# Two networks on one core: TensorE waits for turned columns by halves, for the last turned hidden chunk at the last down slab, and takes the second token tile first in the first down slab

## The chip, the cores and the metric

The kernel runs on one NeuronCore of a Trainium2 chip. The metric is the device time of one execution in microseconds (us); less is better. Engines are named as in the profile: PE is TensorE's matmul, PEld its weight load, DVE is VectorE, ACT is ScalarE, POOL is GpSimd, SP is SyncE, which issues most of the DMAs.

## What is computed

Two residual networks, one after the other, over 256 tokens of width 1024, all in float32. The first has two layers: layer 0 mixes with differential attention and a Fourier branch over latent and context tokens, layer 1 with a gated depthwise convolution. Each is followed by a gated feed-forward network, and shifts, scales and gates come from a condition vector (`ada_w`). The second network has two layers of feed-forward, mixer (short convolution, gated linear recurrence, forgetting attention), feed-forward. What matters here are the six feed-forward networks (width 2816) and the way from each residual sum to the next product:

```python
x = x + gate * swiglu(modulate(rmsnorm(x, g), shift, scale), w1, w3, w2)   # first network, x2
x = x + 0.5 * swiglu_2(rms_norm(x, g), w_in, w_out)                        # second network, x4
def swiglu(h, w1, w3, w2):
    return (jax.nn.silu(h @ w1) * (h @ w3)) @ w2
```

## The kernel before, in words

**Slabs and threes.** All dense weights pass through SBUF as 258 slabs of 128x2048 numbers, in one fixed order. SP loads slab g into one of 5 `raw` buffers as soon as that buffer's last slab has been used up. ACT rounds it to the short format fp32r (`hi`, line 1285), DVE takes the rest (`lo` = raw - hi, line 1803), both into a ring of 4. The split of slab d waits for the semaphore `used` of slab d-4. A product is three matmuls of 512 columns (lines 459 to 461, or 790, 791 and 793 in the down products): hi weights by hi rows, lo by hi, hi by lo. So the rows that are multiplied must be split too: into XTh and XTl (normed input, turned, so that channels lie on the partitions) or HTh and HTl (turned hidden).

**Places.** p = 0 to 9 numbers the residual sums. `down(p)` makes the sums of place p, and the up products of place p read their normed result. There are 256 tokens in two tiles, t = 0 and 1, of 128. An up slab has half of the 1024 input channels for 512 output columns, so a chunk c of 256 hidden columns (gate and up side by side) takes two slabs, 24 matmuls each: 4 blocks of channels, 2 tiles, 3 matmuls. A feed-forward has 11 chunks (NC = 11), 22 up slabs and 11 down slabs; a down slab also has 24 matmuls.

**The up stage** (`ffn`, from line 879). PE multiplies chunk c into banks 0 and 1 or 2 and 3, and between its two slabs turns chunk c-1's hidden rows into bank 4 (`turn_chunk`, line 888, four transposes). ACT makes silu of the gate (line 1566), DVE the hidden product (lines 2238, 2240). From the turned bank ACT makes HTh (line 1546) and DVE HTl (line 1890); the semaphores are `ht_hi` and `ht_lo`. In `down` the sums lie in banks 4 and 5 for tile 0 and in banks 6 and 7 for tile 1 (`acc`), so bank 4, the turning bank, must be free: before the down stage PE waits for `ht_lo` of chunk 9. In down slab 0 it multiplies tile 0 and then tile 1; then `late` turns chunk 10 into bank 2 and waits for its `ht_lo`, although chunk 10 is read only by down slab 10. ACT and DVE have their part of `late` ahead of the split of down slab 4.

**The end of a down stage** (line 804 on). The last three slabs are multiplied for tile 0 first, so DVE can add tile 0's residual while PE does tile 1 of them. DVE and ACT norm the rows, PE turns them (`turn`, line 773), DVE scales them into FULL in two halves of 4 channel blocks (line 2167 or 2170), and ACT and DVE split each half into XTh (line 1301) and XTl (line 1890), with the semaphores `xt_hi` and `xt_lo` for place, tile and half. Then the next up stage begins: in `first_chunks` (places 0 to 3) with two chunks for tile 0, `turn(p, 1)` among them, then both for tile 1; in `first_chunk` (places 4 to 8) with one chunk. Both wait for both halves of a tile's columns before the first product of it, though half 0 of a chunk's slabs reads only half 0 of the columns.

**Other work in the first feed-forward.** In places 0 and 2 the ada weights for later shifts and gates are also loaded through `raw`, quarter by quarter, and DVE sums them over channels into ROW (lines 1837 and 1840, four instructions a quarter). Two quarters later PE turns a half of such a row (`half_turn`, line 518) and DVE stores it (lines 1852 to 1857). In the down stage of the first feed-forward this goes on in `ada_in_down`, after each slab.

Of the kernel before, what the change touches and what calls it, by code (L numbers as in the profile page):

```python
# [27 lines left out]
NC = KF // 2  # L28
# [56 lines left out]
class Counts:  # L85
# [12 lines left out]
    def up(self, name, key=0, step=1):  # L98
        assert (name, key) not in self.table, (name, key)
        shared = SEMAPHORE.get(name, name)  # L100
        self.n[shared] = self.n.get(shared, 0) + step
        self.table[name, key] = self.n[shared]
        return self.sem(name), step
# [182 lines left out]
def program(nc, A, out, known):  # L286

    ctx = ExitStack()
    with ctx:
        counts = Counts(nc, ctx, known)  # L290
        up, at = counts.up, counts.at
# [160 lines left out]
        def tensor_engine(pe):  # L452
# [150 lines left out]
            d = first["w_in"]  # L603
# [170 lines left out]
                                            IDENT[:, :])  # L774
                    last.then_inc(*up("turned", (p, t, h)))

            def down(p, xh, xl, late, order=None, before=None, after=None):
                nslab, d = DOWNS[p][0], first[f"down{p}"]
                order = order or range(nslab)

                def products(s, t):
                    r = (d + s) % RING
                    for n in range(2):
                        kk = 2 * order[s] + n
                        sh, sl = xh[:, kk, tok[t]], xl[:, kk, tok[t]]
                        w = [(hi[r][:, n * D + m * 512:n * D + m * 512 + 512], lo[r][:, n * D + m * 512:n * D + m * 512 + 512])
                             for m in range(2)]
                        begin, end = s == 0 and n == 0, s == nslab - 1 and n == 1
                        for m in range(2):
                            pe.matmul(acc[t][m][:, :], sh, w[m][0], start=begin, stop=False)  # L790
                            pe.matmul(acc[t][m][:, :], sh, w[m][1], start=False, stop=False)  # L791
                        for m in range(2):
                            last = pe.matmul(acc[t][m][:, :], sl, w[m][0], start=False, stop=end)  # L793
                    return last

                for s in range(1 if p == 0 else 0, nslab - 3):
                    ready(d + s)
                    if before:
                        before(s)
                    products(s, 0)  # L800
                    products(s, 1).then_inc(*up("used", d + s))
                    if late is not None and s == 0:
                        late()
                    if after:
                        after(s)
                for s in range(nslab - 3, nslab):
                    ready(d + s)
                    if before:
                        before(s)
                    last = products(s, 0)  # L810
                    if p == 0 and s == 1:
                        late()
                last.then_inc(*up("summed", p))
                products(nslab - 3, 1).then_inc(*up("used", d + nslab - 3))
                if p < 9 and not normed_first(p):
                    turn(p, 0)
                products(nslab - 2, 1).then_inc(*up("used", d + nslab - 2))
                if normed_first(p):
                    turn(p, 0)
                products(nslab - 1, 1).then_inc(*up("used", d + nslab - 1))  # L820

            def first_chunk(p):

                d = first[f"up{p}"]

                def products(half, t):
                    r = (d + half) % RING
                    for k in range(4):
                        kk = 4 * half + k
                        last = three(bank[t][:, :], XTh[:, kk, tok[t]], XTl[:, kk, tok[t]],  # L830
                                     hi[r][:, k * CH:(k + 1) * CH], lo[r][:, k * CH:(k + 1) * CH], kk == 0, kk == KD - 1)
                    return last

                ready(d)
                pe.wait_ge(*at("xt_hi", (p, 0, 1)))
                pe.wait_ge(*at("xt_lo", (p, 0, 1)))
                products(0, 0)
                turn(p, 1)
                ready(d + 1)
                products(1, 0)  # L840
                pe.wait_ge(*at("xt_hi", (p, 1, 1)))
                pe.wait_ge(*at("xt_lo", (p, 1, 1)))
                products(0, 1).then_inc(*up("used", d))
                products(1, 1).then_inc(*up("used", d + 1))

            def first_chunks(p, between, after):


                d = first[f"up{p}"]

                def products(c, half, t):
                    r = (d + 2 * c + half) % RING
                    for k in range(4):
                        kk = 4 * half + k
                        last = three(bank[2 * c + t][:, :], XTh[:, kk, tok[t]], XTl[:, kk, tok[t]],
                                     hi[r][:, k * CH:(k + 1) * CH], lo[r][:, k * CH:(k + 1) * CH], kk == 0, kk == KD - 1)
                    return last

                pe.wait_ge(*at("xt_hi", (p, 0, 1)))
                pe.wait_ge(*at("xt_lo", (p, 0, 1)))  # L860
                for c in range(2):
                    for half in range(2):
                        ready(d + 2 * c + half)
                        products(c, half, 0)
                        if (c, half) == (1, 0):
                            turn(p, 1)
                            after()
                pe.wait_ge(*at("xt_hi", (p, 1, 1)))
                pe.wait_ge(*at("xt_lo", (p, 1, 1)))
                for c in range(2):  # L870
                    products(c, 0, 1).then_inc(*up("used", d + 2 * c))
                    if c:
                        between()
                    products(c, 1, 1).then_inc(*up("used", d + 2 * c + 1))

            def x_groups(c):
# [2 lines left out]
            def ffn(p):  # L879
                f, d = FFNS[p], first[f"up{p}"]  # L880

                def turn_chunk(c, b):
                    pe.wait_ge(*at("hidden", (f, c, 1)))
                    if c:
                        pe.wait_ge(*at("ht_lo", (f, c - 1)))
                    for k in range(2):
                        for t in range(T):
                            last = pe.transpose(b[:, k * S + t * P:k * S + (t + 1) * P], HID[:, t, k * P:(k + 1) * P],  # L888
                                                IDENT[:, :])
                    last.then_inc(*up("hid_turned", (f, c)))  # L890

                def ada_sums(c):

                    gates, shifts = halves_of(FFN_ADA[p][c - 2])
                    for l, mod, h in gates:
                        pe.wait_ge(*(at("added", (p, 1)) if h else at("xt_lo", (p, 1, 1))))
                        half_gate(l, mod, h, bank[5 + h])
                    for l, mod, h in shifts:
                        pe.wait_ge(*at("added", (p, 1)))
                        half_turn(l, mod, h, bank[7])  # L900

                if normed_first(p):
                    first_chunks(p, lambda: turn_chunk(0, bank[4]), lambda: None)
                else:
                    first_chunk(p)
                for c in range(2 if normed_first(p) else 1, NC):
                    if c >= 2:
                        pe.wait_ge(*at("hidden", (f, c - 2, 1)))
                    half_chunk(d + 2 * c, 0, x_groups(c))
                    turn_chunk(c - 1, bank[4])  # L910
                    if p in SHIFTED:
                        ada_sums(c)
                    half_chunk(d + 2 * c + 1, 1, x_groups(c))
                pe.wait_ge(*at("ht_lo", (f, NC - 2)))

                def late():
                    turn_chunk(NC - 1, bank[2])
                    pe.wait_ge(*at("ht_lo", (f, NC - 1)))

                def ada_in_down(s):  # L920

                    for l, mod, h in halves_of(FFN_ADA[0][NC - 2 + s] if s < 2 else DOWN_ADA[s - 2])[1]:
                        half_turn(l, mod, h, bank[1])

                if p in SHIFTED:
                    pe.wait_ge(*at("gate_full", (*FFN_GATE[p], 1)))
                if p == 0:
                    pe.wait_ge(*at("mods", (1, 1, 0, "full")))
                down(p + 1, HTh, HTl, late, after=ada_in_down if p == 0 else None)

            def before_w_out(s):

# [1908 lines left out]
```

## Time and profile before

| | before |
|---|---|
| median of 3 runs | 1772.92 us (1772.43 to 1774.08) |
| profiled execution, span from first to last instruction | 1771.1 us |
| PE busy | 1696.4 us, 96% |
| PEld, DVE, ACT, POOL busy | 1370.1, 1104.2, 807.9, 48.2 us |
| instructions | 20813 |
| DMA | 332.29 MB, mean 188 GB/s |

The time of the profiled execution is given by its span; the median of the runs is 1.8 us above that. Busy time is the sum of the stretches in which an engine ran an instruction; the idle time before an instruction is put down to what released it. Matmuls overlap in the profile (one lasts 0.39 us, but starts come 0.23 us apart), so starts are compared below, not ends.

### The profile page before, as it was taken

How to read it: one execution, taken by the hardware profiler on the slowest of the kernel's cores; microseconds unless marked ns; L12 is line 12 of the kernel's file. 1: busy time of each engine (PE TensorE's matmuls, PEld its weight loads, DVE VectorE, ACT ScalarE, POOL GpSimd, SP SyncE). 2: the span in 40 equal slices, each digit the busy share in tenths (PEclk: the TensorE clock that was granted, in tenths of full speed). 3: DMA queues.
4: the chain of work that ended last, by engine and by line, in shares of the span. 5: the costliest groups of instructions: out<-in, count | busy, mean ns of one | idle time of the engine just before them, and what ended most of it. 6: DMA issues, size and time to landing. Idle time of an engine off the chain costs nothing.

```text
span 1771.1 us, 20813 instructions
## 1 busy us (share of the span) xinstructions
PE 1696.4 (96%) x8168; PEld 1370.1 (77%) x8168; DVE 1104.2 (62%) x1284; ACT 807.9 (46%) x970; POOL 48.2 (3%) x60
## 2 busy tenths in 40 slices
PE   6999899998988999999999999999999999999999
PEld 3775678787656887788787888887888778888877
DVE  3876788877767664655547856554655458755542
ACT  3425544423445443454436555443444346664441
POOL 0001000000000000000001200000000003000000
PEclk9999999999989999999999999999999999999999
DMA  9683288887434765565555427655565454336550
GB/s 354 223 290 113 89 286 281 307 290 257 159 102 152 240 238 179 166 197 184 185 166 167 152 67 212 190 190 177 180 190 190 168 168 164 119 108 210 185 187 25
DMA packets 239985, 332.29 MB, mean 188 GB/s; under 512 B 11024, under 2 KB 191988, under 8 KB 239888
## 3 DMA queue, kind: packets, MB, share of 16 engines
q1 hardware_dynamic: 235872, 321.95, 55.0%
q10 hardware_dynamic: 2704, 5.82, 0.9%
q0 software_dynamic: 1312, 3.19, 0.7%
q8 instruction: 66, 1.08, 0.3%
q14 instruction: 31, 0.25, 0.0%
HBM read 329.87 MB, written 1.05 MB: 187 GB/s over the span
## 4 chain that ended last, share of the span: by engine, by line
PE 84%; DVE 9%; ACT 3%; issue 2%; DMA 1%; SPq 0%; DVEq 0%; ACTq 0%
PE bank L459 17%; PE bank L461 17%; PE bank L460 17%; PE bank L790 7%; PE bank L793 7%; PE bank L791 7%; DVE lo L1803 3%; PE bank L888 2%; DMA raw<-in_ada_w 1%; ACT hi L1285 1%; PE bank L773 1%; PE bank L1229 1%; PE bank L1230 1%; PE bank L1232 1%; PE bank L950 1%
## 5 line engine op out<-in xcount | busy, mean ns | idle before, releaser
L1803 DVE TENSOR_TENSOR lo<-raw,hi 128x2048 fp32r<-128x2048 f32 x258 | 591.2, 2295 | 382.1 <-ACT hi L1285 381.8
L1285 ACT ACTIVATE hi<-raw 128x2048 fp32r<-128x2048 f32 x258 | 491.6, 1911 | 335.5 <-PE bank L461 174.9
L459 PE MATMUL bank<-hi,XTh 128*128 128x512 f32 (+1 forms) x1424 | 564.7, 397 | 9.5 <-ACT XTh L1301 3.0
L461 PE MATMUL bank<-hi,XTl 128*128 128x512 f32 (+1 forms) x1424 | 553.3, 389 | 0.0
L460 PE MATMUL bank<-lo,XTh 128*128 128x512 f32 (+1 forms) x1424 | 552.9, 388 | 0.0
L459 PEld LDWEIGHTS bank<-hi,XTh 128*128 128x128 f32 x1424 | 268.8, 189 | 70.8 <-issue 6.2
L461 PEld LDWEIGHTS bank<-hi,XTl 128*128 128x128 f32 x1424 | 268.3, 188 | 56.0
L460 PEld LDWEIGHTS bank<-lo,XTh 128*128 128x128 f32 x1424 | 268.8, 189 | 52.7 <-issue 1.0
L790 PE MATMUL bank<-hi,HTh 128*128 128x512 f32 x528 | 208.5, 395 | 9.3 <-DVE HTl L1890 9.3
L791 PE MATMUL bank<-lo,HTh 128*128 128x512 f32 x528 | 206.6, 391 | 0.0
L793 PE MATMUL bank<-hi,HTl 128*128 128x512 f32 x528 | 164.0, 392 | 0.0
L790 PEld LDWEIGHTS bank<-hi,HTh 128*128 128x128 f32 x528 | 100.0, 189 | 31.5 <-DVE HTl L1890 11.0
L793 PEld LDWEIGHTS bank<-hi,HTl 128*128 128x128 f32 x528 | 99.7, 189 | 21.0
L791 PEld LDWEIGHTS bank<-lo,HTh 128*128 128x128 f32 x528 | 100.0, 189 | 20.4
L1566 ACT ACTIVATE SG<-bank,ST 128x256 f32<-128x256 f32 x88 | 36.9, 470 | 136.5 <-PE bank L461 136.5
L1840 DVE SCALAR_TENSOR_TENSOR ROW<-raw,CS,ROW 128x512 f32<-128x512 f32 x126 | 94.6, 751 | 4.2
L1301 ACT ACTIVATE XTh<-FULL 128x512 fp32r<-128x512 f32 x44 | 27.4, 632 | 103.2 <-DVE FULL L2170 67.2
L2240 DVE SCALAR_TENSOR_TENSOR HID<-bank,ST,SG 128x256 f32<-128x256 f32 x88 | 38.5, 478 | 55.6 <-ACT SG L1566 55.6
L1890 DVE TENSOR_TENSOR HTl<-bank,HTh 128x512 fp32r<-128x512 f32 x66 | 45.1, 684 | 9.1 <-ACT HTh L1546 9.1
L1566 ACT ACTIVATE SG<-bank 128x256 f32<-128x256 f32 x44 | 14.5, 382 | 71.2 <-PE bank L461 71.2
L1546 ACT ACTIVATE HTh<-bank 128x512 fp32r<-128x512 f32 x66 | 38.5, 583 | 16.3 <-PE bank L888 16.3
L2683 POOL TENSOR_TENSOR hg_e<-hg_BC 128x256 f32<-128x256 f32 x12 | 23.3, 1942 | 635.7 <-DVE hg_BC L2533 615.4
(363 smaller groups left out, 1412.0 us busy)
## 6 DMA issues: line engine op xcount, KB each, us to landing
raw<-in_ffn_w_in SPq DMA_DIRECT2D x176, 512.0 KB, 4.9
raw<-in_ffn_w SPq DMA_DIRECT2D x132, 512.0 KB, 4.9
raw<-in_ada_w SPq DMA_DIRECT2D x96, 512.0 KB, 5.0
raw<-in_ffn_w_out SPq DMA_DIRECT2D x88, 512.0 KB, 4.0
raw<-in_w_mix_in SPq DMA_DIRECT2D x52, 512.0 KB, 4.7
raw<-in_od_pw_w SPq DMA_DIRECT2D x24, 512.0 KB, 5.3
raw<-in_ev_w_in SPq DMA_DIRECT2D x20, 512.0 KB, 9.4
raw<-in_w_mix_out SPq DMA_DIRECT2D x16, 512.0 KB, 3.8
```

Source lines behind the costliest of these rows:

```text
L459: pe.matmul(dst, xh, wh, start=start, stop=False)
L460: pe.matmul(dst, xh, wl, start=False, stop=False)
L461: return pe.matmul(dst, xl, wh, start=False, stop=stop)
L790: pe.matmul(acc[t][m][:, :], sh, w[m][0], start=begin, stop=False)
L791: pe.matmul(acc[t][m][:, :], sh, w[m][1], start=False, stop=False)
L793: last = pe.matmul(acc[t][m][:, :], sl, w[m][0], start=False, stop=end)
L1285: act.activation(hi[r][:, :], raw[g % RAW][:, :], ACT.Copy).then_inc(*up("hi", d))
L1546: act.activation(HTh[:, 2 * c:2 * c + 2, :], b[:, :].rearrange("p (k s) -> p k s", k=2), ACT.Copy).then_inc(*up("ht_hi", (f, c)))
L1566: act.activation(SG[:, t, :], bank[2 * (c % 2) + t][:, 0:HALF], ACT.Silu, scale=1.0 if p in SHIFTED else ST[:, t:t + 1]).then_inc(*up("gat ...
L1803: dve.tensor_tensor(lo[r][:, :], raw[g % RAW][:, :], hi[r][:, :].bitcast(F32), ALU.subtract).then_inc(*up("lo", d))
L1840: m = dve.scalar_tensor_tensor(out=part, in0=w[:, k, :], scalar=CS[:, kk, 0:1], in1=part, op0=ALU.mult, op1=ALU.add)
L1890: dve.tensor_tensor(dst, src, h.bitcast(F32), ALU.subtract).then_inc(*up(name, i))
```

## The change

`down` gets a hook `head`: with it, slab 0 multiplies tile 1, calls the hook, then multiplies tile 0. The feed-forwards give it the wait for chunk 9's `ht_lo`, which stood before `down`. The wait for chunk 10's `ht_lo` leaves `late` and stands before down slab 10. `columns_ready` waits for one half of one tile's columns, and `first_chunk` and `first_chunks` call it before the first product that reads the half. Only PE's program changes.

```diff
-            def down(p, xh, xl, late, order=None, before=None, after=None):
+            def down(p, xh, xl, late, order=None, before=None, after=None, head=None):
...
-                    products(s, 0)
-                    products(s, 1).then_inc(*up("used", d + s))
+                    if head is not None and s == 0:
+                        products(s, 1)
+                        head()
+                        products(s, 0).then_inc(*up("used", d + s))
+                    else:
+                        products(s, 0)
+                        products(s, 1).then_inc(*up("used", d + s))
...
+            def columns_ready(p, t, half):
+
+                pe.wait_ge(*at("xt_hi", (p, t, half)))
+                pe.wait_ge(*at("xt_lo", (p, t, half)))
+
             def first_chunk(p):
...
                 ready(d)
-                pe.wait_ge(*at("xt_hi", (p, 0, 1)))
-                pe.wait_ge(*at("xt_lo", (p, 0, 1)))
+                columns_ready(p, 0, 0)
                 products(0, 0)
                 turn(p, 1)
                 ready(d + 1)
+                columns_ready(p, 0, 1)
                 products(1, 0)
-                pe.wait_ge(*at("xt_hi", (p, 1, 1)))
-                pe.wait_ge(*at("xt_lo", (p, 1, 1)))
+                columns_ready(p, 1, 0)
                 products(0, 1).then_inc(*up("used", d))
+                columns_ready(p, 1, 1)
                 products(1, 1).then_inc(*up("used", d + 1))
...
-                pe.wait_ge(*at("xt_hi", (p, 0, 1)))
-                pe.wait_ge(*at("xt_lo", (p, 0, 1)))
                 for c in range(2):
                     for half in range(2):
                         ready(d + 2 * c + half)
+                        if c == 0:
+                            columns_ready(p, 0, half)
                         products(c, half, 0)
...
-                pe.wait_ge(*at("xt_hi", (p, 1, 1)))
-                pe.wait_ge(*at("xt_lo", (p, 1, 1)))
                 for c in range(2):
+                    if c == 0:
+                        columns_ready(p, 1, 0)
                     products(c, 0, 1).then_inc(*up("used", d + 2 * c))
                     if c:
                         between()
+                    else:
+                        columns_ready(p, 1, 1)
                     products(c, 1, 1).then_inc(*up("used", d + 2 * c + 1))
...
-                pe.wait_ge(*at("ht_lo", (f, NC - 2)))
+
+                def turn_bank_free():
+                    pe.wait_ge(*at("ht_lo", (f, NC - 2)))
 
                 def late():
                     turn_chunk(NC - 1, bank[2])
-                    pe.wait_ge(*at("ht_lo", (f, NC - 1)))
+
+                def last_hidden(s):
+                    if s == NC - 1:
+                        pe.wait_ge(*at("ht_lo", (f, NC - 1)))
...
-                down(p + 1, HTh, HTl, late, after=ada_in_down if p == 0 else None)
+                down(p + 1, HTh, HTl, late, before=last_hidden, after=ada_in_down if p == 0 else None,
+                     head=turn_bank_free)
```

## Rows read from the trace of the kernel before

**Rows 1.** The page's first part: busy time and share of each engine.
```profile
PE 1696.4 (96%) x8168; PEld 1370.1 (77%) x8168; DVE 1104.2 (62%) x1284; ACT 807.9 (46%) x970; POOL 48.2 (3%) x60
```
**Rows 2.** Waits of PE, all of the run: who for whom, us, times, longest.
```profile
PE bank L790 <- DVE HTl L1890: 9.3, 6, 2.2
...
PE bank L459 <- ACT XTh L1301: 3.0, 3, 1.0
...
PE bank L459 <- DVE XTl L1890: 2.6, 2, 1.5
```
**Rows 3.** Timeline of PE, third feed-forward: start us, us, what, [idle before <-releaser].
```profile
868.02 0.39 PE L790 MATMUL bank<-hi,HTh 128*128 128x512 f32 x1
...
873.47 0.60 PE L888 MATMUL bank<-IDENT,HID 128*128 128x128 f32 x4
875.48 0.50 PE L790 MATMUL bank<-hi,HTh 128*128 128x512 f32 x1 [1.41 <-DVE HTl L1890]
```
**Rows 4.** Timeline of PE, chunks turned without a wait after them.
```profile
330.44 0.60 PE L888 MATMUL bank<-IDENT,HID 128*128 128x128 f32 x4
330.87 0.95 PE L518 MATMUL bank<-ONES,ROW 128*128 128x2 f32 x8
...
1083.59 0.60 PE L888 MATMUL bank<-IDENT,HID 128*128 128x128 f32 x4
1083.94 0.48 PE L459 MATMUL bank<-hi,XTh 128*128 128x512 f32 x1
```
**Rows 5.** Timeline of PE, second feed-forward, around `late`.
```profile
680.48 0.50 PE L790 MATMUL bank<-hi,HTh 128*128 128x512 f32 x1 [1.48 <-DVE HTl L1890]
```
**Rows 6.** Timeline of PE, first feed-forward, from the last up product to down slab 2.
```profile
348.36 0.39 PE L461 MATMUL bank<-hi,XTl 128*128 128x512 f32 x1
350.95 0.50 PE L790 MATMUL bank<-hi,HTh 128*128 128x512 f32 x1 [2.21 <-DVE HTl L1890]
...
358.15 0.60 PE L888 MATMUL bank<-IDENT,HID 128*128 128x128 f32 x4
360.17 1.05 PE L518 MATMUL bank<-ONES,ROW 128*128 128x2 f32 x8 [1.41 <-DVE HTl L1890]
361.08 0.48 PE L790 MATMUL bank<-hi,HTh 128*128 128x512 f32 x1
...
368.24 0.95 PE L518 MATMUL bank<-ONES,ROW 128*128 128x2 f32 x8
```
**Rows 7.** Timeline of DVE, the same stretch.
```profile
350.22 0.68 DVE L1890 TENSOR_TENSOR HTl<-bank,HTh 128x512 fp32r<-128x512 f32 x1
...
351.48 2.28 DVE L1803 TENSOR_TENSOR lo<-raw,hi 128x2048 fp32r<-128x2048 f32 x1
353.68 3.10 DVE L1840 SCALAR_TENSOR_TENSOR ROW<-raw,CS,ROW 128x512 f32<-128x512 f32 x4
```
**Rows 8.** Stretches: us, PE, PEld, DVE, ACT, POOL busy, PEclk, DMA share, GB/s.
```profile
352.10:355.50 3.40, 3.40 (x10) 2.62 (x9) 3.33 (x4) 0.65 (x2) 0.00 (x0) 0.50 1.07 382
...
362.40:365.80 3.40, 3.40 (x10) 2.66 (x9) 3.29 (x6) 0.00 (x0) 0.00 (x0) 0.50 0.30 48
...
499.00:512.50 13.50, 8.49 (x24) 5.15 (x23) 7.30 (x13) 9.39 (x21) 0.00 (x0) 0.50 0.29 91
550.10:556.90 6.80, 5.48 (x17) 4.72 (x18) 5.16 (x13) 2.26 (x3) 0.00 (x0) 0.50 0.49 157
748.10:751.50 3.40, 3.40 (x13) 3.01 (x13) 2.85 (x15) 0.80 (x2) 0.00 (x0) 0.50 0.95 290
```
**Rows 9.** Timeline of PE, start of the up products of place 1.
```profile
426.61 0.47 PE L459 MATMUL bank<-hi,XTh 128*128 128x512 f32 x1 [0.54 <-DVE lo L1803]
...
434.24 1.09 PE L773 MATMUL bank<-IDENT,XN 128*128 128x128 f32 x8 [1.90 <-DVE XN L2156]
...
439.12 0.47 PE L459 MATMUL bank<-hi,XTh 128*128 128x512 f32 x1 [1.04 <-DVE XTl L1890]
```
**Rows 10.** Timeline of DVE, place 1: the two halves of tile 1's XTl.
```profile
437.50 1.48 DVE L1890 TENSOR_TENSOR XTl<-FULL,XTh 128x512 fp32r<-128x512 f32 x2
```

## The prediction

> **What bounds the kernel now.** I read the busy shares first: PE 96%, DVE 62% [rows 1]. So time comes off only where PE stands still or runs at its lower clock. The list of PE's waits comes next. HTl, which the first two edits concern, costs 9.3 us in six waits of a down product [rows 2], and 1.4 us in one of line 518 [rows 6]; XTh and XTl, the third edit's, cost 3.0 and 2.6 us [rows 2]. That makes at most 10.7 + 5.6 us of idle time. Third come the timelines at these places, which show what is late next, and last the stretches with the granted clock, which is half (1.2 GHz for 2.4) in some of them [rows 8].
>
> **Edit 1: chunk 10's wait moves from `late` to down slab 10.** In the third feed-forward line 888 starts at 873.47 and the next product at 875.48, 2.01 us; where nothing is waited for it is 0.35 us [rows 3, 4]. The wait costs 1.66 us. The six waits of 9.3 us [rows 2] are this one four times (third to sixth feed-forward, 1.41 each), 1.48 in the second [rows 5] and 2.21 of edit 2: so 4 x 1.66 = 6.64, and 1.73 in the second. In the first, 358.15 to 360.17 is 2.02, less 0.43, the distance of such a pair in its up stage: 1.59 [rows 4, 6].
> What is late next? Down slabs 1 to 3 were split before or during slab 0, and slab 4 is needed three slabs later (5.45 us each, 868.02 to 873.47 [rows 3]). DVE and ACT keep their order, HTl comes first, and it is ready some 40 us before slab 10. Nothing is queued behind the moved wait that needs it earlier.
>
> **Edit 2: tile 1 first, the bank's wait behind it.** It matters only where chunk 9's HTl is late: in the first feed-forward, where the quarters of ada keep DVE busy. There 348.36 to 350.95 is 2.59 us between starts for 0.23 of a steady stream: 2.36 us lost [rows 6]. Now tile 1's 12 matmuls start at about 348.6 and last 2.7, to 351.3, and HTl is finished at 350.90 [rows 7]: all 2.36 us are covered, with 0.4 to spare. In the other five HTl was there already: nothing.
> What the first feed-forward then meets: the turn of chunk 10 comes at about 354.0, and chunk 10's HID is made right behind HTl, before 351.48 [rows 7]. Line 518 follows at 354.5; its row was summed in the up stage. The next line 518, after slab 1, comes at 354.04 + 0.43 + 0.91 + 5.45 = 360.8. It needs the quarter that ends at 356.78 [rows 7], and that DVE has stored the half before: HTl (0.7) from 356.8, `lo` of slab 4 (2.3), two small ones to about 360.1. Only 0.7 us to spare, but enough. From there each DVE step hangs on PE's `used` or on a quarter as before, only earlier.
>
> **Term 3: the clock behind these two stalls.** In the first feed-forward the granted clock is 0.50 from 352.1 to 355.5 and from 362.4 to 365.8 [rows 8]. Slab 0 takes 350.95 to 358.15 = 7.20 us and slab 1 361.08 to 368.24 = 7.16 us [rows 6], against 5.45 at the full clock [rows 3]: 1.75 + 1.71 = 3.46 us. Each fall follows a stall that the edits remove: 2.2 us of idle time, then 1.4 us with the eight tiny matmuls of line 518. Bounds: 0 (both stay or fall elsewhere) and 3.46. I take 3.46, since in the up stage the same pair of lines 888 and 518 without a stall [rows 4] brings no fall.
>
> **Edit 3: columns by halves.** Tile 0 waits at places 0, 1 and 2, three times 1.0 us [rows 2]. With half 0 alone PE starts 0.8 us sooner, but the second slab's products still wait for `lo` (426.61 at place 1), and the turn of tile 1 for XN, with 1.90 us idle [rows 9]. Both are made by DVE, which nothing there makes faster. So this is nothing, at places 0 and 2 too. Places 3 to 8 begin without a stall: nothing. What is left is tile 1 of place 1: PE stands 1.04 us before 439.12 [rows 9], the two halves of XTl take 1.48 from 437.50 [rows 10], the first of them 0.68; it is ready at 438.18, plus the 0.14 that also lies between 438.98 and 439.12: start at 438.32, 0.80 us sooner. What follows (`used`, the split, the biased rows, the gated rows that PE waits for) starts from PE's own signals and comes as much sooner. Bounds: 0 and 1.04; I take 0.80. The extra waits, four in each of nine places, are already satisfied or are those above. Streams that cross slabs, with two to four waits in them, still show 0.23 us between starts, so I count them at nothing; at a guessed upper bound of 0.05 each, 1.8 us.
>
> **The sum.** 6.64 + 1.73 + 1.59 + 2.36 + 3.46 + 0.80 = 16.6 us. The profiled execution's span of 1771.1 becomes 1754.5; the median lies 1.8 above the span, so **1756.3**.
>
> **Rival 1: the clock's low stretches move instead of going.** For it: the falls don't follow stalls in a fixed way. 1.4 us of idle time brings one at 362.4, and the same 1.4 us in the third to sixth feed-forward brings none; others last 3.4 us at 748, 6.8 at 550 and 13.5 at 499, the convolution's end [rows 8]. All that comes after the first feed-forward now comes some 7 us sooner, so the remaining stalls can meet other luck. Against it: at both places the stall itself is gone. It takes 3.46 back: **1759.8**. The Trainium skill (TensorE: Matmul & The Clock Gate, "What's actually happening") says that the monitor behind the clock runs freely and isn't reset when a kernel starts; by that rule falls are drawn anew in each execution, also those at 550 and 748, either way. The trace agrees as far as one trace can: equal stalls, unequal falls.
>
> **Rival 2: the first feed-forward's down stage becomes DVE's or the DMA's.** DMA share is 1.07 at 382 GB/s in 352.1 to 355.5 [rows 8], and a slab with its quarter costs DVE 2.3 + 3.1 of 5.9 us. If PE's lead of 7.4 us (2.36 + 1.59 + 3.46) is taken back there, the time is 1772.9 - 9.2 = **1763.7**. Against it: in 362.4 to 365.8 the DMA share is only 0.30, because SP waited for buffers that DVE freed late; that slack moves the loads forward too.
>
> **Rival 3: the edits do less than they say**, for instance because `late`'s wait is replaced at once by one for slab 1's `lo`, or tile 1 first must wait for banks 6 and 7. Then edit 1's 10.0 us stay: 1772.9 - 6.6 = **1766.3**. Against it: PE waits nowhere for a down slab's `lo` except at places' starts.
>
> **Rival 4, slower: the clock gives out at the starts of places 0 to 3 and in the convolution's end.** Edit 3 gathers idle time: at place 1, 0.99 + 0.54 us become one short stall and one of 1.3 us between small groups of matmuls. If that lets the clock fall there, a low stretch of 3.4 us costs about 1.7 (term 3's 1.75 and 1.71). With those of the first feed-forward kept, 13.1 us of gain are left, so eight more turn the sign, and eleven, 18.7 us, give 1772.9 - 13.1 + 18.7 = **1778.5**. The low stretches listed [rows 8] last 30.5 us, nine such, and PE's idle places at the four starts and in the convolution don't offer room for eleven more.
>
> **How the numbers follow.** Forecast with all terms 0.60, within 1.7 us of 1756.3, a low stretch more or less; rival 1 0.24; rival 2 0.06; rival 3 0.03; rival 4 0.02. The rest, 0.05, is that low stretches at 550 and 748 vanish as well: 1756.3 - 3.4 = 1752.9. The range from 1752.6 to 1761.5 holds the forecast, the last case and rival 1 with a stretch more (1759.8 + 1.7); rivals 2 to 4 stay out. About 0.2%, or 3.5 us, can be told from no change here. All cases but rival 4 are faster by more than that; small mishaps together get 0.02 for no difference.
>
> **What would show it.** In the profile after: no wait of lines 790 and 518 for HTl; starts of line 888 and the next product 0.35 apart in all down stages; slab 0 of the first feed-forward straight after the last up product, and 24 matmuls in 5.45 us there; PEclk 1.00 there; XTl's wait at place 1 down to about 0.2 us; XN's wait at places 0, 1 and 2 at the same end, with longer idle time before `lo`. I am wrong if a new wait of PE over 1 us stands between down slabs, if the first feed-forward's down stage is no 7 us shorter, or if the low stretches add up to as much as before.

## The result, and the profile after

The changed kernel takes 1756.74 us (median of 4 runs, 1754.35 to 1758.85), the one before 1773.50 (4 runs, 1772.43 to 1774.78). The ratio is 0.9906, with a 95% interval of 0.9895 to 0.9918. The forecast was 1756.3. The profiled execution is the slowest of the four: 1758.85 us, with a span of 1757.5.

The page's first part after the change answers to [rows 1]:

```profile
PE 1693.4 (96%) x8168; PEld 1369.7 (78%) x8168; DVE 1104.6 (63%) x1284; ACT 807.5 (46%) x970; POOL 48.1 (3%) x60
```

The same 8168 matmuls are busy 3 us less, and the span is 13.6 us shorter. The waits of PE (who for whom: us, times, longest) answer to [rows 2]:

```profile
PE bank L773 <- DVE XN L2174: 8.6, 4, 3.4
...
PE bank L459 <- ACT hi L1303: 3.8, 3, 1.3
...
PE bank L459 <- DVE XTl L1908: 2.9, 5, 1.6
...
PE bank L773 <- DVE X L2171: 2.8, 2, 2.5
...
PE bank L900 <- DVE HID L2258: 1.6, 1, 1.6
```

HTl is gone from the list, all 10.7 us of it. Of the columns' waits, 5.6 us before, 2.9 are left, but a new line stands there: 3.8 us for ACT's `hi` (whose `lo` follows), where before `lo` itself had 2.1. The waits for XN are as long as they were.

The timeline of PE in the first feed-forward, from the last up product (350.34) to down slab 2 (start us, us, what), answers to [rows 6]. Line 888 of before is line 900 now:

```profile
350.34 0.39 PE L461 MATMUL bank<-hi,XTl 128*128 128x512 f32 x1
350.57 0.39 PE L790 MATMUL bank<-hi,HTh 128*128 128x512 f32 x1
...
356.01 0.60 PE L900 MATMUL bank<-IDENT,HID 128*128 128x128 f32 x4
356.45 0.95 PE L518 MATMUL bank<-ONES,ROW 128*128 128x2 f32 x8
357.26 0.48 PE L790 MATMUL bank<-hi,HTh 128*128 128x512 f32 x1
...
362.81 0.95 PE L518 MATMUL bank<-ONES,ROW 128*128 128x2 f32 x8
```

No wait is left, and slab 0 takes 356.01 - 350.57 = 5.44 us instead of 7.20. DVE in the same stretch, which answers to [rows 7]:

```profile
352.21 0.68 DVE L1908 TENSOR_TENSOR HTl<-bank,HTh 128x512 fp32r<-128x512 f32 x1
...
355.67 3.10 DVE L1858 SCALAR_TENSOR_TENSOR ROW<-raw,CS,ROW 128x512 f32<-128x512 f32 x4
358.69 0.69 DVE L1908 TENSOR_TENSOR HTl<-bank,HTh 128x512 fp32r<-128x512 f32 x1
359.30 2.28 DVE L1821 TENSOR_TENSOR lo<-raw,hi 128x2048 fp32r<-128x2048 f32 x1
```

Chunk 9's HTl ends at 352.89, and tile 0's products could start at 350.57 + 2.72 = 353.29: covered, with the 0.4 us to spare that the prediction gave. Chunk 10's HTl ends at 359.38, 2.9 us after line 518, where PE used to wait for it.

In the third feed-forward the turn of chunk 10 and the next product are now 0.35 us apart, which answers to [rows 3]:

```profile
866.54 0.60 PE L900 MATMUL bank<-IDENT,HID 128*128 128x128 f32 x4
866.89 0.48 PE L790 MATMUL bank<-hi,HTh 128*128 128x512 f32 x1
```

At place 1 edit 3 did this (PE's timeline), which answers to [rows 9]:

```profile
416.89 0.47 PE L459 MATMUL bank<-hi,XTh 128*128 128x512 f32 x1 [0.24 <-DVE XTl L1908]
...
421.15 0.47 PE L459 MATMUL bank<-hi,XTh 128*128 128x512 f32 x1 [1.27 <-ACT hi L1303]
...
428.83 1.74 PE L773 MATMUL bank<-IDENT,XN 128*128 128x128 f32 x8 [2.00 <-DVE XN L2174]
430.22 0.78 PE L459 MATMUL bank<-hi,XTh 128*128 128x512 f32 x1
```

The first wait is 0.75 us shorter, the second 0.73 longer, and that for XN within 0.1 us of what it was. The matmul at 430.22 lasts 0.78 us, where one at the full clock lasts 0.48 (as at 866.89): the clock is low here. The stretches (us; PE, PEld, DVE, ACT and POOL busy; PEclk, DMA share, GB/s) answer to [rows 8]:

```profile
350.00:363.00 13.00, 13.00 (x67) 10.93 (x65) 12.82 (x16) 6.35 (x7) 0.00 (x0) 1.00 1.00 360
...
429.10:432.50 3.40, 3.40 (x13) 2.93 (x12) 2.74 (x9) 0.70 (x2) 0.00 (x0) 0.50 0.98 357
494.00:507.60 13.60, 8.41 (x24) 5.25 (x24) 7.19 (x13) 9.60 (x21) 0.00 (x0) 0.50 0.24 81
545.20:552.00 6.80, 5.62 (x18) 4.75 (x19) 5.02 (x13) 2.40 (x3) 0.00 (x0) 0.50 0.47 157
740.00:745.00 5.00, 3.79 (x20) 3.00 (x20) 4.35 (x18) 1.42 (x4) 0.00 (x0) 1.00 0.76 245
```

The first down stage runs at the full clock throughout. The low stretch at place 3 (748 before) is gone, and a new one stands at place 1.

**The account of the two profiles**, from the same instructions' starts in both. PE begins to turn tile 1 at place 0 2.0 us later (227.27 against 225.31); what edit 3 gained at tile 0 there, the next wait had taken back. The 2.0 us were lost before 40 us had passed, where both kernels run the same instructions. Then come, as gains: 2.37 (bank's wait), 1.76 (slab 0's clock), 1.58 (chunk 10's wait), 1.61 (slab 1's clock), 1.73 in the second feed-forward, and 1.66, four times. That is 15.7 us. Place 1, with its new low stretch, loses 0.3. 15.7 - 2.0 - 0.3 = 13.4, against 13.6 in the spans.

### The profile page after: what moved, and what is told of

It is laid out like the page before. It is cut to its first block, busy times and chain, and to the rows that moved or that the text cites. A ratio compares the mean times of both kernels' runs of the same rounds, so it can differ in the third digit from the quotient of the medians.

```text
span 1757.5 us, 20829 instructions
## 1 busy us (share of the span) xinstructions
PE 1693.4 (96%) x8168; PEld 1369.7 (78%) x8168; DVE 1104.6 (63%) x1284; ACT 807.5 (46%) x970; POOL 48.1 (3%) x60
## 3 DMA queue, kind: packets, MB, share of 16 engines
q0 software_dynamic: 1312, 3.19, 0.7%
## 4 chain that ended last, share of the span: by engine, by line
PE 85%; DVE 8%; ACT 3%; issue 2%; DMA 1%; SPq 0%; DVEq 0%; ACTq 0%
PE bank L459 17%; PE bank L461 17%; PE bank L460 17%; PE bank L790 7%; PE bank L791 7%; PE bank L793 7%; DVE lo L1821 3%; PE bank L900 2%; DMA raw<-in_ada_w 1%; ACT hi L1303 1%; PE bank L773 1%; PE bank L1247 1%; PE bank L1248 1%; PE bank L1250 1%; PE bank L968 1%
## 5 line engine op out<-in xcount | busy, mean ns | idle before, releaser
L900 PE MATMUL bank<-IDENT,HID 128*128 128x128 f32 x264 | 39.6, 272 | 1.6 <-DVE HID L2258 1.6
```

## The experiments

The first four variants ran on one chip, the last four on another, each time with the kernel before beside them: 1773.22 us on the first chip, 1774.28 on the second. A variant's median is of 4 to 11 runs.

**Edit 1 alone, on the kernel before.**

```diff
                 def late():
                     turn_chunk(NC - 1, bank[2])
-                    pe.wait_ge(*at("ht_lo", (f, NC - 1)))
+                def last_hidden(s):
+                    if s == NC - 1:
+                        pe.wait_ge(*at("ht_lo", (f, NC - 1)))
...
-                down(p + 1, HTh, HTl, late, after=...)
+                down(p + 1, HTh, HTl, late, before=last_hidden, after=...)
```

> The kernel before with edit 1 alone (chunk 10's wait moved from late to down slab 10). Theory (stalls plus the clock behind them): the third to sixth feed-forward give 1.66 us each, the second 1.73, the first 1.59, together 10.0 us, and the granted clock's low stretch behind the first feed-forward's late (1.7 us) goes as well; the stall of 2.2 us at the bank's wait and the low stretch behind it stay. 1773.5 - 11.7 = 1761.8 us. Rival 1 (low stretches are drawn anew and do not belong to the stalls): the profile shows low stretches in the first down stage or elsewhere as before, 1763.5 us, and their number differs between the kernels of this call without a pattern. Rival 3 (the wait is replaced at once by one for a slab's lo): PE waits behind line 888, and the time stays above 1770 us.

Measured: 1761.96 us, ratio 0.9937 (0.9924 to 0.9949). PE waits for HTl once more, 2.2 us, and the stretches around it show the clock:

```profile
348.00:352.80 4.80, 2.60 (x12) 1.87 (x11) 4.76 (x6) 2.65 (x4) 0.00 (x0) 1.00 1.00 347
352.80:356.20 3.40, 3.40 (x9) 2.63 (x9) 3.37 (x4) 1.30 (x2) 0.00 (x0) 0.50 1.01 392
356.20:367.00 10.80, 10.80 (x59) 9.15 (x58) 6.78 (x10) 2.85 (x3) 0.00 (x0) 1.00 0.69 226
```

The first low stretch follows the stall that was kept; the second is gone with the stall that was taken out. Against the trace of before the steps are 1.58 + 1.61 + 1.73 + 4 x 1.66 = 11.6 us. The theory holds by the trace. The time alone doesn't decide it: its interval, 9.1 to 13.5 us, also holds the 1763.5 us of rival 1. Rival 3 falls as far as it concerns `late`, since nothing replaces the wait there.

**Edit 2 alone, on the kernel before.**

```diff
-                    products(s, 0)
-                    products(s, 1).then_inc(*up("used", d + s))
+                    if head is not None and s == 0:
+                        products(s, 1)
+                        head()
+                        products(s, 0).then_inc(*up("used", d + s))
...
-                pe.wait_ge(*at("ht_lo", (f, NC - 2)))
+                def turn_bank_free():
+                    pe.wait_ge(*at("ht_lo", (f, NC - 2)))
```

> The kernel before with edit 2 alone (tile 1 first in down slab 0, the bank's wait behind it). Theory: only the first feed-forward's stall of 2.2 us goes, worth 2.36 us, and with it the low clock stretch in slab 0, 1.75 us; the five other feed-forwards start slab 0 as before. The late wait and the low stretch behind it stay. 1773.5 - 4.1 = 1769.4 us. Rival 1: 2.4 us, 1771.1 us, with the low stretch still in slab 0. A rival for the hardware: the order of tiles itself costs or gives something, which would show as down slab 0 taking other than 5.45 us in the third to sixth feed-forward.

Measured: 1768.79 us, ratio 0.9978 (0.9969 to 0.9986), so 2.5 to 5.5 us. The median is as expected, the account behind it is not. Slab 0 starts 0.23 us after the last up product and takes 5.44 us in all six feed-forwards, so the order of the tiles costs nothing, and no wait for banks 6 and 7 comes in. PE's timeline around `late` in the first feed-forward, and the stretches:

```profile
354.88 0.60 PE L893 MATMUL bank<-IDENT,HID 128*128 128x128 f32 x4
358.29 1.06 PE L518 MATMUL bank<-ONES,ROW 128*128 128x2 f32 x8 [2.82 <-DVE HTl L1898]
```

```profile
350.00:354.90 4.90, 4.90 (x24) 3.99 (x23) 4.90 (x6) 3.58 (x5) 0.00 (x0) 1.00 1.02 364
355.00:359.20 4.20, 1.38 (x13) 1.15 (x12) 4.09 (x6) 2.40 (x2) 0.00 (x0) 1.00 0.99 350
359.20:362.60 3.40, 3.40 (x10) 2.72 (x10) 3.29 (x6) 0.00 (x0) 0.00 (x0) 0.50 0.99 351
```

DVE's timeline says why the wait has grown from 1.41 to 2.82 us:

```profile
354.53 3.10 DVE L1848 SCALAR_TENSOR_TENSOR ROW<-raw,CS,ROW 128x512 f32<-128x512 f32 x4
357.55 0.68 DVE L1898 TENSOR_TENSOR HTl<-bank,HTh 128x512 fp32r<-128x512 f32 x1
```

PE turns chunk 10 at 354.88, but DVE is in a quarter of ada until 357.63 and makes HTl only then. Of 2.37 + 1.76 = 4.13 us, 1.40 are given back at `late`: 2.7 us by the trace. This profile's span is 4.1 us shorter, and the clock elsewhere has its part in that: at place 2 the low stretch of before (550.1 to 556.9) is missing, though PE waits for XN as long as before (3.40 us for 3.38), and that gives 1.3 us by the starts. Whether the median's excess has the same cause wasn't shown. In the changed kernel the same quarter still delays HTl, but nobody waits for it.

**Edit 3 alone, on the kernel before** (the diff's `columns_ready` and its calls, nothing else).

> The kernel before with edit 3 alone (columns waited for by halves). Theory as predicted: 0.8 us at place 1's second tile, nothing else: 1772.7 us. What the trace after suggests: tile 0 at places 0, 1 and 2 starts 0.75 us sooner and the next wait, for the second slab's lo, is 0.75 us longer; at place 1 the 0.8 us comes only in an execution whose clock is at its full rate there. So between 0 and 0.8 us, 1772.7 to 1773.5 us. Rival: extra waits cost 0.05 us each, 1.8 us: 1775.3 us.

Measured: 1771.97 us, ratio 0.9993 (0.9984 to 1.0002): no difference that can be told in the time. The trace tells it. PE at place 1:

```profile
435.76 1.09 PE L773 MATMUL bank<-IDENT,XN 128*128 128x128 f32 x8 [1.98 <-DVE XN L2163]
436.61 0.47 PE L459 MATMUL bank<-hi,XTh 128*128 128x512 f32 x1
...
439.85 0.47 PE L459 MATMUL bank<-hi,XTh 128*128 128x512 f32 x1 [0.23 <-ACT XTh L1308]
```

The clock is full here, and the wait before tile 1 falls from 1.04 to 0.23 us. Line 974 of before (the taps, behind it) is 0.80 us nearer, the size that was predicted. At places 0, 1 and 2 tile 0 starts some 0.7 us sooner, and the next wait is as much longer. The extra waits cost nothing visible. Both low stretches of the first down stage are there, after both stalls, though they start at other times:

```profile
353.50:357.00 3.50, 3.50 (x10) 2.76 (x9) 3.43 (x4) 0.71 (x2) 0.00 (x0) 0.51 1.05 375
...
363.80:367.20 3.40, 3.40 (x9) 2.63 (x8) 3.29 (x6) 0.00 (x0) 0.00 (x0) 0.50 0.25 48
```

**Edits 1 and 2 without edit 3.** The changed kernel with `first_chunk` and `first_chunks` as before.

> The changed kernel without edit 3 (edits 1 and 2 alone). Theory: edits 1 and 2 are the whole gain but for at most 0.8 us: 1756.7 to 1757.5 us, with no low clock stretch in the first feed-forward's down stage, 12.3 us of stalls and 3.4 us of low clock gained. If the terms do not add (the clock's part counted twice), the gains of e1_late and e2_head add up to 2 us more or less than this kernel's.

Measured: 1758.90 us, ratio 0.9919 (0.9906 to 0.9933), so 11.9 to 16.7 us. The median lies 1.4 us above the range that was expected. By the trace the steps are 2.37, 1.76, 1.58, 1.61, 1.73 and 4 x 1.66, together 15.7 us, with no low stretch in the first down stage. By the trace they add to more than the parts: in the first feed-forward edit 1 alone gives 1.58 + 1.61 = 3.19, edit 2 alone 2.73, both 7.32. The missing 1.40 us is the quarter on DVE, which bites only when PE both comes early and waits. The medians can't show this: the gains of the two alone, 11.3 and 4.4 us, come to 15.7, those of both to 14.3, with intervals some 3 to 5 us wide.

The profile also tells whose the low stretch at place 1 is. It is here without edit 3, behind the same wait for XN:

```profile
428.97 1.69 PE L773 MATMUL bank<-IDENT,XN 128*128 128x128 f32 x8 [1.93 <-DVE XN L2167]
```

```profile
429.30:432.70 3.40, 3.40 (x13) 2.92 (x12) 2.85 (x9) 0.81 (x2) 0.00 (x0) 0.50 0.99 349
```

The 0.3 us that place 1 loses are here as well. So neither comes from edit 3, under which alone the clock stayed full there.

**What is left: DVE's chain at the places' starts.** The waits for XN (8.6 us) and for X before line 773 (3.2 us at places 4, 6 and 7) didn't move. DVE idles 1.2 us for ACT's `hi` ahead of two splits, and makes tile 1's residual only behind them. Two orders on DVE, alone and together, on the changed kernel:

```diff
-            def residual(p, t):
+            def residual(p, t, parts=(0, 1), add=True):
...
                 else:
+                    early = {0: (0, 1), 1: (0, 1), 2: (0,), 3: (0, 1)}.get(p, ())
+                    if early:
+                        residual(p, 1, early, False)
                     split(d + nslab - 3 + RING)
+                    if not two_first(p):
+                        rows(p, 1, tuple(n for n in (0, 1) if n not in early))
                     split(d + nslab - 2 + RING)
-                    rows(p, 1)
+                    if two_first(p):
+                        rows(p, 1, tuple(n for n in (0, 1) if n not in early))
```

With `add=False`, `residual` makes only the products with the gate for the halves in `parts`, and the sum follows where it stood. The lines with `early` are the first order (places 0 to 3), `if not two_first(p)` is the second (places 4, 6, 7 and 9).

> The changed kernel, and on DVE at places 0 to 3 the products of tile 1's sums with the gate (two instructions of 0.68 us, 1.3 us together; at place 2 one of the two bias and gate pairs, 1.4 us) stand ahead of the two splits, where DVE idles 1.2 us for ACT's hi. Theory (what edit 3 gives back is given back to DVE's chain, residual, norm, turn): XN or X for the turn of tile 1 comes about 1.2 us sooner at each of the four places, PE's wait there falls from 2.0, 2.0, 3.4 and 2.5 us by that much, 4.8 us at most, against 0.1 to 0.2 us later lo at each: 1756.7 - 4.2 = 1752.5 us. Rival: ACT's hi and the squares set it, or the tile's columns are next in line, and PE's waits only change their name: 1756 to 1757 us.

> The changed kernel, and on DVE at places 4, 6 and 7 (and 9) the residual of tile 1 (two instructions, 1.3 us) stands between the two splits of the down stage's end instead of behind both. Theory: PE's three waits of 1.05 us for X before line 773 go, the second split is needed only a chunk later: 1756.7 - 3.1 = 1753.6 us. Rival: DVE must wait for the last product anyway (used comes when the first split ends), or the second split's slab is now late: 1756 to 1757 us, with a wait for lo at the next chunk.

> Both of these DVE orders on the changed kernel. Theory: they touch different places, so the gains add: 1756.7 - 4.2 - 3.1 = 1749.4 us. Rival: 1756 to 1757 us, as above.

> The changed kernel once more, on the chip of the three others, as their base: 1756.7 us within 1.5. Theory for the clock: no low stretch in the first feed-forward's down stage (the stalls are gone), the one or two at the starts of places 0, 1 and 3 there or not. Rival 1: a low stretch in that down stage in this execution.

Measured on one chip: the changed kernel 1759.29 us, a ratio to the kernel before of 0.9920 (0.9905 to 0.9935), 2.6 us above what was expected of it; gate products first 1747.96; residual between the splits 1753.56; both 1743.74, with a ratio to the kernel before of 0.9833 (0.9818 to 0.9847). Against the changed kernel the first order gives 11.3 us where 4.2 were expected, the second 5.7 for 3.1. So **both together beat the changed kernel by 15.6 us**, twice what was expected. PE's waits with both:

```profile
PE bank L773 <- DVE XN L2177: 4.6, 4, 2.1
...
PE bank L459 <- ACT hi L1303: 3.8, 3, 1.3
...
PE bank L773 <- DVE X L2174: 1.5, 2, 1.2
```

XN's waits are 4.0 us shorter, 1.3 at each of three places, the wait for X at place 3 is 1.3 us shorter, and the three for X at places 4, 6 and 7 are gone (steps of 1.23, 1.22 and 1.21). That is 9.0 us, 1.7 more than the 7.3 expected. At place 3 0.5 us is lost just before, where the first product of the up stage stands 0.91 us for 0.40; the profile names no releaser there, and the cause stays open. Small drifts take 0.1 more. DVE at place 0, with the gate's two products in its idle time at 214.00:

```profile
212.60 1.48 DVE L1908 TENSOR_TENSOR XTl<-FULL,XTh 128x512 fp32r<-128x512 f32 x2
214.00 1.28 DVE L2153 TENSOR_TENSOR XN<-bank,GATE 128x512 f32<-128x512 f32 x2
215.29 4.50 DVE L1821 TENSOR_TENSOR lo<-raw,hi 128x2048 fp32r<-128x2048 f32 x2
219.71 1.22 DVE L2160 TENSOR_TENSOR X<-X,XN 128x1024 f32<-128x1024 f32 x1
```

The rest is the clock. It is full at places 0, 1 and 2, where the changed kernel's profiles have low stretches of 3.4, 3.4 and 6.8 us:

```profile
224.00:230.00 6.00, 5.73 (x28) 4.62 (x29) 3.93 (x10) 2.75 (x4) 0.00 (x0) 1.00 0.75 252
423.00:430.00 7.00, 6.62 (x32) 5.36 (x33) 4.02 (x11) 1.26 (x2) 0.00 (x0) 1.00 1.00 372
...
537.00:545.00 8.00, 7.43 (x36) 5.99 (x37) 4.21 (x11) 3.22 (x5) 0.00 (x0) 1.00 0.42 142
```

By the starts of the same instructions this gives 1.1, 1.1 and 2.1 us, and a shorter low stretch at the convolution's end (10.2 us for 13.7) another 0.9: 5.2 us in all. 2.0 us of the two profiles' difference lies before place 0 again: 9.0 - 0.6 + 5.2 + 2.0 = 15.6, as in the spans.

Do the shorter stalls keep the clock full? The executions speak for it: the mean granted clock is 0.993 or 0.994 in all eight with the gate products first, and at most 0.992 in every other one recorded. But a low stretch can also be missing where the stall is whole. With the residual between the splits PE waits 1.96 us for XN at place 0, as in the changed kernel, and the clock stays full, which is 1.1 us of what this order gained:

```profile
226.55 1.09 PE L773 MATMUL bank<-IDENT,XN 128*128 128x128 f32 x8 [1.96 <-DVE XN L2174]
```

```profile
226.50:230.70 4.20, 3.91 (x21) 3.09 (x21) 3.35 (x10) 1.38 (x3) 0.00 (x0) 1.00 0.85 262
```

Among the eight profiles with the old order at the gate, the low stretch is missing in three at place 0, in four at place 1 and in one at place 2; in the two with the new order it is missing at all three. So the longer stalls seem to make a low stretch more likely there, but don't settle it.

## Why the prediction was right

**Edit 1** (6.64 + 1.73 + 1.59): measured 6.64, 1.73 and 1.58, in the changed kernel and alone. That HTl would be there in time held too: no wait stands before down slab 10.

**Edit 2** (2.36): 2.37, from the first feed-forward alone, with the predicted 0.4 us to spare. The second use of line 518 found its half stored as well: DVE ends it at 361.84, PE comes at 362.81, with 1.0 us to spare for the 0.7 predicted. What I had not seen is that a third of edit 2's gain (1.40 of 4.13 us, its clock term included) hangs on edit 1.

**The clock behind the stalls** (3.46): 1.76 + 1.61 = 3.37. The prediction set slab 1's 7.16 us against 5.45, but with the turned half in it slab 1 takes 5.55 at the full clock (357.26 to 362.81), hence 1.61 for 1.71. Here I chose the upper bound, and the runs bear it out. The kernels before and with edit 3 keep both stalls and show both low stretches, edit 1 alone keeps the first stall and its stretch, edit 2 alone the second and its stretch, and six profiles without the stalls (the changed kernel's two, edits 1 and 2, and the three with new orders) show none there. So **rival 1 falls for this place**. It holds for others: the low stretch at place 1 is in the profile of edits 1 and 2 and not in that of before, and the one at place 3 the other way round, though at both places the stalls before the stretch are the same within 0.1 us. The executions show it too: the four runs of the changed kernel have spans of 1757.5, 1753.1, 1755.7 and 1755.2 us at mean granted clocks of 0.988, 0.992, 0.989 and 0.990. The monitor's free run, as the Trainium skill (TensorE: Matmul & The Clock Gate, "What's actually happening") states it, fits this. Why 1.4 us of idle time brought a fall in the first down stage and none in the third to sixth feed-forward stays open; the eight tiny matmuls of line 518 beside it were not tried by themselves.

**Edit 3** (0.80): right in size and place where the clock is full (edit 3 alone, 0.80), and nothing in the changed kernel's own profile. There the clock was low from 429.1 to 432.5, so PE came to tile 1 when its columns were ready, and place 1 as a whole lost 0.3 us, as it did without edit 3. So this term of the sum gave nothing in the profiled execution. That it gives nothing at tile 0 was right three times. The prediction had no stall at place 3; there edit 3 halves a wait for XTl that comes once the clock is full (0.62 us for 1.21 with edits 1 and 2 alone), and the wait for HID behind it takes that back (1.59 for 0.99).

**The sum against the span.** I took 1.8 us between span and median. The run of span 1757.5 took 1758.85, so 1.35 lie outside the span; the other 0.4 was that profile's luck. By spans alone the gain is 13.6, not 16.6: the second profile lost 2.0 us before place 0, edit 3's 0.8 were missing, and place 1 lost 0.3. Over the runs it is 16.8, and on the second chip it was 15.0 (1774.28 to 1759.29). So the mechanisms were right and worth 15.7 us by the trace, but that the forecast came within 0.5 us of the median is luck.

**Rivals 2 to 4.** DVE and DMA kept up in the first down stage, at a DMA share of 1.00 over 13 us, with no wait of PE. Rival 3 is refuted by edit 1 alone for `late`, and by edit 2 alone for the banks. Rival 4 blamed edit 3's gathered idle time, and there is a low stretch at place 1, one and not eight; but it is there without edit 3 and not there with edit 3 alone, so in these profiles it isn't edit 3's.

## What to carry to other kernels

Put each wait in front of the first instruction that reads the data, and order independent work so that what is ready goes first; the price of the wait is then the distance between starts beside the same pair without a wait. Do it for the whole chain at once: here, by the trace, one edit alone gave part of its gain to the next wait, and with both it was whole. Where the data are late because the engine that makes them is behind (XN here), moving the reader's waits gives nothing; the order of the maker's work does, here 15.6 us, as much as the three edits together (15.0 on the same chip).

## What the hardware showed that I had not expected

A short stall can cost twice. In the first down stage 4.0 us of stalls cost 3.4 us more in slower matmuls behind them. At places 0 to 2, with stalls shorter by 1.3 us, the clock stayed at 2.4 GHz in both profiles, where it had fallen to 1.2 in the changed kernel's two, and the new orders gained about 5 us beyond their waits. I had left that out of their expectations.

A low clock can also cost nothing. At place 3, where PE was 6.75 us ahead of the profile of before, the full clock put it 8.4 us ahead at the end of tile 0's products (753.05 before, 744.66 after). Of these 1.6 us a new wait for tile 1's XTl took 0.8, and a wait for HID of 1.59 us instead of 0.80 the other 0.8 (PE's timeline after the change):

```profile
745.67 0.47 PE L459 MATMUL bank<-hi,XTh 128*128 128x512 f32 x1 [0.62 <-DVE XTl L1908]
...
755.67 0.66 PE L900 MATMUL bank<-IDENT,HID 128*128 128x128 f32 x4 [1.59 <-DVE HID L2258]
```

The first 40 us, in which PE's longest waits are for loads of the ada weights (7.2 us for one, before), differ by 2 us between two executions of the same code. In the stretch from 20 to 38 the granted clock was 0.81 before and 0.72 after. Why it differs there wasn't tried.
